# One transfer per 32 rows for an attention component's operands, and five adaLN blocks preloaded ahead of attention

## The reference, cut to what matters

```python
mod = silu(c) @ w_ada + b_ada                      # 6 x 1024 per sequence: "adaLN"
sh1, sc1, g1, sh2, sc2, g2 = split(mod, 6)
h   = rmsnorm(x, norm1_g) * (1 + sc1) + sh1
mix = concat[retention(h), forgetting_attention(h), differential_attention(h)]
x   = x + g1 * (mix @ w_out)
h   = rmsnorm(x, norm2_g) * (1 + sc2) + sh2
x   = x + g2 * (relu(h @ w_up) ** 2 @ w_down)

# differential attention, 6 heads of 2 x 32 query/key dimensions, both rotated (rope: halves of 16)
p = softmax(q[c] @ k[c].T / sqrt(32) + mask)       # c = 0, 1
a = p[0] - lam * p[1]
out = a @ v
```

## Time and profile before

| | us |
|---|---|
| median of three runs | 3327.64 |
| the profiled execution: own time | 3326.87 |
| the profiled execution: span, first to last instruction | 3325.1 |
| PE busy in it | 3224.1 (97%) |
| VectorE busy | 1696.0 (51%) |
| ScalarE busy | 984.5 (30%) |
| GpSimd busy | 957.8 (29%) |

### The profile page before, as it was taken

One profiled execution on the slowest core, in us unless ns is written; L12 is line 12 of the kernel. 1 busy time (PEld: TensorE's weight loads), 2 busy tenths in 40 slices (PEclk: granted clock), 3 DMA queues, 4 the chain that ended last, 5 costly groups with the idle time before them and its releaser, 6 DMA issues.

```text
span 3325.1 us, 50329 instructions
## 1 busy us (share of the span) xinstructions
PE 3224.1 (97%) x19286; PEld 2894.2 (87%) x19286; DVE 1696.0 (51%) x3073; ACT 984.5 (30%) x1770; POOL 957.8 (29%) x690
## 2 busy tenths in 40 slices
PE   6999999899999999999999999999999999999998
PEld 3988897566799999999988879966678999999997
DVE  4746273674495555555573544156546633333335
ACT  3132222574451111111232313147635311111112
POOL 1312332221232333333332214212213233333332
PEclk8999999999999999999999999999999999999999
DMA  5512476535112222222222114563321011111112
GB/s 213 180 47 95 156 238 218 125 91 139 33 59 85 85 76 76 88 82 82 83 64 73 35 50 176 190 172 76 76 66 45 27 51 44 44 45 50 44 44 72
DMA packets 135351, 307.07 MB, mean 92 GB/s; under 512 B 53789, under 2 KB 74341, under 8 KB 131729
## 3 DMA queue, kind: packets, MB, share of 16 engines
q1 hardware_dynamic: 93584, 224.39, 23.4%
q10 hardware_dynamic: 41600, 80.44, 6.9%
HBM read 240.14 MB, written 57.90 MB: 90 GB/s over the span
## 4 chain that ended last, share of the span: by engine, by line
PE 90%; DVE 4%; SPq 2%; ACT 1%; ACTq 1%; issue 1%; DMA 1%; DVEq 0%
PE ps L1387 22%; PE ps L1358 19%; PE ps L1299 9%; PE ps L1232 8%; PE ps L1022 6%; PE ps L1212 5%; PE ps L1078 4%; PE ps L1169 3%; PE ps L1276 3%; PE ps L1004 2%; PE ps L1046 1%; DVE tn L2053 1%; PE ps L1334 1%; DVE h_lo L2066 1%; DVE x L2238 1%; PE ps L1113 1%
## 5 line engine op out<-in xcount | busy, mean ns | idle before, releaser
L768 POOL CAST w_hi<-raw 128x1024 fp32r<-128x1024 f32 x212 | 229.5, 1082 | 1862.5 <-PEq L1393 447.3
L2238 DVE SCALAR_TENSOR_TENSOR x<-ps,mod,x 128x352 f32<-128x352 f32 (+2 forms) x768 | 353.6, 489 | 431.5 <-PE ps L1387 351.5
L1387 PE MATMUL ps<-act_hi,w_hi 128*128 128x352 f32 x1536 | 496.0, 323 | 0.0
L1387 PE MATMUL ps<-act_hi,w_lo 128*128 128x352 f32 x1536 | 492.6, 321 | 0.0
L1387 PE MATMUL ps<-act_lo,w_hi 128*128 128x352 f32 x1536 | 492.1, 320 | 0.0
L1358 PE MATMUL ps<-h_hi,w_hi 128*128 128x352 f32 x1344 | 433.5, 323 | 0.0
L1875 ACT ACTIVATE relu_b<-ps,consts 128x352 f32<-128x352 f32 x192 | 106.4, 554 | 1103.5 <-PE ps L1358 1084.3
L1358 PE MATMUL ps<-h_hi,w_lo 128*128 128x352 f32 x1344 | 430.8, 320 | 0.0
L1358 PE MATMUL ps<-h_lo,w_hi 128*128 128x352 f32 x1344 | 430.4, 320 | 0.0
L1299 PE MATMUL ps<-pT,vb 128*128 128x512 f32 (+5 forms) x1080 | 401.3, 461 | 0.0
L2302 DVE TENSOR_REDUCE pm<-ps 128x1 f32<-128x512 f32 (+4 forms) x468 | 251.2, 548 | 243.3 <-PE ps L1169 158.8
(11 more groups left out here) (223 smaller groups left out, 6112.3 us busy)
## 6 DMA issues: line engine op xcount, KB each, us to landing
raw<-in_w SPq DMA_DIRECT2D x212, 512.0 KB, 3.6
ada_next<-in_w_ada SPq DMA_DIRECT2D x48, 512.0 KB, 4.2
ada_w<-in_w_ada SPq DMA_DIRECT2D x24, 512.0 KB, 5.9
kb<-scr_k SPq DMA_DIRECT2D x36, 328.0 KB
kb<-scr_k SPq DMA_DIRECT2D x120, 82.0 KB
qb<-scr_q SPq DMA_DIRECT2D x36, 264.0 KB
ada_nat<-in_w_ada_first SPq DMA_DIRECT2D x8, 1024.0 KB, 20.5
qb<-scr_q SPq DMA_DIRECT2D x120, 66.0 KB
```

What stands on the lines that cost most here:

```text
L768: pool.tensor_copy(hi, raw[:, uc % 2, 0:width]).then_inc(pool_hi, 1)
L1387: last = mm(ps[:, i % 6, 0:GW], w[:, k * 256 + o * 128:k * 256 + o * 128 + 128], (act_lo if low else act_hi)[:, k * T + g * GW:k * T + (g ...
L2238: last = v.scalar_tensor_tensor(xs, ps[:, bank, a - g * GW:b - g * GW], gs, xs, ALU.mult, ALU.add)
```

## The change

```diff
-STACK_DMAS = {2: 14, 1: 9}
+STACK_DMAS = {2: 8, 1: 9}
...
-ADA_AFTER = {11: range(8, 10), 12: (10,), 13: (11,), 14: range(12, 19)}
+ADA_AFTER = {11: range(8, 10), 12: (10,), 13: (11,), 14: range(12, 19), 16: range(19, 22)}
...
-                    def part(src, which, y):
-                        r = 64 * y + 16 * a
-                        return src[n, which, r:r + 16]
+                    def part(src, which):
+                        return src[n, which].rearrange("(y b r) t -> b y r t", y=2, b=4)[a]
...
-                    for y in range(2):
-                        r = 16 * y
-                        sp.dma_start(k[r:r + 16, :].bitcast(F32), part(scr_k, 0, y)).then_inc(sem, 16)
-                        sp.dma_start(k[32 + r:48 + r, :].bitcast(F32), part(scr_k, 1, y)).then_inc(sem, 16)
-                        sp.dma_start(k[64 + r:80 + r, :].bitcast(F32), part(scr_k, 0, y)).then_inc(sem, 16)
-                        sp.dma_start(q[r:r + 16, 0:T].bitcast(F32), part(scr_q, 0, y)).then_inc(sem, 16)
-                        sp.dma_start(q[32 + r:48 + r, 0:T].bitcast(F32), part(scr_q, 0, y)).then_inc(sem, 16)
-                        sp.dma_start(q[64 + r:80 + r, 0:T].bitcast(F32), part(scr_q, 1, y)).then_inc(sem, 16)
+                    def rows32(buf, r, w):
+                        return buf[r:r + 32, 0:w].bitcast(F32)
+
+                    sp.dma_start(rows32(k, 0, NKEY), part(scr_k, 0)).then_inc(sem, 16)
+                    sp.dma_start(rows32(k, 32, NKEY), part(scr_k, 1)).then_inc(sem, 16)
+                    sp.dma_start(rows32(k, 64, NKEY), part(scr_k, 0)).then_inc(sem, 16)
+                    sp.dma_start(rows32(q, 0, T), part(scr_q, 0)).then_inc(sem, 16)
+                    sp.dma_start(rows32(q, 32, T), part(scr_q, 0)).then_inc(sem, 16)
+                    sp.dma_start(rows32(q, 64, T), part(scr_q, 1)).then_inc(sem, 16)
...
-                    if li == 0 and u < 8:
-                        sp.wait_ge(ada_done, 2 * (19 + u) + 2)
-                        back_load(24 + u)
+                    if li == 0 and u < 5:
+                        sp.wait_ge(ada_done, 2 * (22 + u) + 2)
+                        back_load(27 + u)
```

## The result

| | before | after |
|---|---|---|
| median of the runs, us | 3327.32 (3326.74 to 3330.47, 4 runs) | 3494.49 (3491.3 to 3498.27, 4 runs) |
| the profiled execution: span | 3325.1 | 3489.5 |
| PE busy in it | 3224.1 (97%) | 3257.2 (93%) |
| mean granted clock | 0.985 | 0.965 |

The ratio is 1.0501, with a 95% interval from 1.0483 to 1.0519: the changed kernel is 5% slower. Forecast were 3448 us and slower; direction and mechanism are right, the size is not: +164.4 between the two spans where the sum gave +120.8.

What follows compares the result with a forecast made beforehand. PE, busy 97%, was taken to bound the kernel, its standstills and lower clock moving the end. Projections +46.2, layer 0 +35.8 and layer 1 +38.8 gave +120.8 us on 3326.87: 3448 us, range 3375 to 3545.

Steps and rivals of the forecast that it cites:

- Two engines: Operand loads of the differential components: each new transfer runs on two of 16 DMA engines, 26.4 GB/s each.
- Term 1: End of the projections, both layers: weight unit 32 lands late behind operands, PE waits 23.1 us a layer, +46.2 in all.
- Term 2: First wait of attention: component 2's operands land late, a wait of 15.6 us in place of 5.3, +10.3 a layer.
- Term 3: Components 3 to 11: nine periods at 18.0 or 18.7 us in place of 14.3, +33.3 in layer 1, +39.6 in layer 0.
- One sign: Attention: PE would wait at L1169 for `kb`/`qb` in each of components 2 to 11.
- the values: Value loads in attention: 656 KB every fourth component, 1/16 on each engine, priced at 0.4 us a component.
- The clock: Attention: PE's lower-clock losses after the old waits would come back as gains, 4.8, 2.2 and 2.0 us.
- Part 2: The adaLN preload, layer 0: blocks 24 to 26 loaded early remove a 9.9 us wait and 2 us of lower clock.
- block 27: An adaLN load in layer 0's attention, needed in component 5, when the queue has just passed it; no cost priced.
- The first: Rival on the operand transfers: all 16 engines carry them, so issue time counts, -27.5, 3299 us; chance 0.12.
- the third rival: Component 2's wait stays since stores fill the engines, only the adaLN wait goes, -12, 3315 us; chance 0.03.
- The second: Rival in attention: two engines, ScalarE's queue held up too, PE waits for exponentials, 3528 us; 0.08 with a still slower engine.

Runs made afterwards that it cites:

- Experiment 1: The changed kernel with the 16 rows of a half outermost on each operand transfer's DRAM side, the two halves inside: 3309.01 us, ratio 0.9949.
- experiment 4: The kernel before, its 16-row operand transfers cut to a DRAM-side outermost count of 8, 4 or 2: 3351.5, 3381.1 and 3534.7 us.
- the doses of 2 and 4: The kernel before, its 16-row operand transfers given a DRAM-side outermost count of 2 or 4: 3534.7 and 3381.1 us.
- Experiment 6: The changed kernel with the value loads of pairs 2 to 5 cut to 16 of 128 rows: 3485.25 us, ratio 1.0476.
- experiment 2: The kernel before with only the adaLN edits: blocks 24 to 26 loaded after weight unit 32, 27 to 31 in the loop: 3325.76 us, ratio 0.9997.
- experiment 3: The changed kernel with the adaLN loads as before, so the merged 32-row transfers alone: 3533.37 us, ratio 1.0624.
- the two better versions: Experiment 1's kernel, 3309.01 us, and the same with ScalarE's last projection stores at slot 10 of component 0 in place of slot 3, 3301.29 us.
- experiment 9: The two better versions with the adaLN lines of the kernel before: 3310.38 us beside 3309.01, and 3312.76 us beside 3301.29.
- experiment 5: The changed kernel with the value loads of pairs 1 to 5 issued by ScalarE's queue in place of SP's: 3552.9 us, ratio 1.0674.

## Why the prediction was right, and where its size was off

**Two engines: right.** A 2 outermost on the DRAM side gives two engines' worth of work, at 27 GB/s each (26.4 were taken from the earlier trace rows, and the 21.1 of the earlier trace rows did not come). Experiment 1 takes the loss away with the order alone, experiment 4 brings it back without the merging. The Trainium skill, "DMA: Bandwidth & Descriptors", section "Why a DMA increments its semaphore by 16 and not by 1", has the rule for it: the largest count up to 16 that divides the slowest dimension of both sides. After, experiment 1 (16 and 32) and the doses of 2 and 4 agree with it; with 8 the engines are not full, so that its time neither bears the rule out nor speaks against it. The advice of the same page's "Rules for kernel authors", to coalesce small transfers, holds here only with the 16 outermost: the same merging gives -17 us with it and +206 without.

**Term 1: right.** 23.1 us were said for each layer, PE waits 24.0 and 24.6; unit 32 was to land at 544.9, and GpSimd starts on it at 545.13. The bounds of 10 and 31 were wider than needed.

**Term 2: right in kind, 4 us short.** A wait of 15.6 was said, 20.05 and 19.97 were measured. ScalarE's stores take more of the engines than the 5.0 us that I read from 8 us of before's queue: from 577 to 610 in after they are 22.2% of 33 us, 7.3 us on each engine. The rest may be the time by which the loads were issued one behind the other; no run separates it.

**Term 3, the period: right.** 18.0 was said, SP issues a component in 17.4 to 17.7. In undisturbed components the lag grows by 2.9 to 3.5 us (layer 1: components 5 to 8), against 3.7 forecast, 0.4 of them for the values. But there are eight such periods and not nine: component 11 adds nothing. The eight are some 25 us of the 59 in layer 1. One sign came otherwise than said: PE does not wait at L1169 in each component, but six times in all. In most components its stops of 1.0 to 2.6 us are at L1276, for row transfers. The loads set the pace even so: the chain of after from 600.17 to 662.95 holds SP's issues of operands and values and then the landing of `qb<-scr_rows` (646.70 to 662.95), and no work of an engine.

**The step that failed: the values.** The prediction says "A share of the values (656 KB every fourth component, 1/16 on each engine) adds 0.4 us": it priced them by bytes, and by a transfer that lands at once. Measured in layer 1, by what each component adds to the lag: component 4, after whose operands the values of pair 1 are issued, 8.9 us; components 9 and 10, at the values of pair 2, 13.9 and 5.7. Over the 3.2 of an ordinary component that is 5.7 and 13.2, 18.9 us a layer, where 3.6 were priced. Layer 1 missed by 59.2 - 38.8 = 20.4 us: 15.3 from the values, 4.8 from the start up to component 2 (4.4 of them the wait of term 2), 4.8 from the clock (below), less 4.5: 3.3 for component 11, and the rest since the other eight were a little cheaper than said. Two causes lie behind the values:
- The load is dearer than its bytes. It is read in pieces of 64 floats, 256 B. Queue of SP in the DMA view of 627 to 642 in after, where pair 1's values are loaded:

```profile
q1 hardware_dynamic: 2482, 1.34, 30.2%
```

  30.2% of 16 engines for 15 us are 72.5 us of engine time. Less 30 for the two that never rest, 42.5 us lie on the other 14: 3.0 us an engine for one load, and not 1.6 (a few constants of the operands are in the sum too). Cutting the loads of pairs 2 and 3 to an eighth gave back 4.0 us from component 0 to 11 of layer 1, and 1.4 in layer 0.
- It lands late. Pair 2's values are issued from 748 on, behind the operands of component 10, and wanted at 755.7, with the last of them landing 17.8 us after the first issue. In before the same six transfers went out from 654.20 and had landed by 660.0, 34 us ahead of PE's use at 694.5. So the lead is gone, and a part of each transfer lies behind a component's worth of operands on two engines: PE stands 10.1 us in layer 0 and 7.2 in layer 1. Experiment 6 shows that this stays with smaller loads and a free SP. It is 7.2 of the 13.2 us of layer 1. The remaining 6.0 go with what follows that stop, a lower clock (0.72 from 745.7 to 776.3 in layer 0) and a wait of 3.8 us for the next row transfer; no run takes them apart, nor the 5.7 us of pair 1, whose loads stayed whole in experiment 6.

**The clock: wrong.** The sum took 9.0 us off (4.8, 2.2 and 2.0), since clock losses would be hidden in stretches that the engines bind. But PE's busy time rose by 33.1 us with the same instructions: behind each wait PE runs at its lower level (1.2 GHz) for a part of the time, and there are many more waits (the granted clock was 0.90 in the steady period and 0.79 from 575 to 600, shown above; 0.985 and 0.965 over the spans). The first matmuls on unit 32 take 0.49 us and not 0.32. Within a late stretch this is hidden; at its start and end it is not: from component 0 to 2 of layer 1 the lag grows by 15.1 us, and the wait alone by 14.6. The 4.8 us are not returned there, nor later, as the rest of the lag is accounted for by the periods.

**Part 2: the forecast of -12 held only in company.** The wait at 600 is gone. Alone the edit gives nothing (experiment 2), beside the merged transfers 39 us (experiment 3), with the two better versions 1.4, within their spread, and 11.5 (experiment 9). What the prediction held hidden, block 27 "when the queue has just passed it", is late by 3.3 us for VectorE and 4.9 for PE: it is issued at 684.87, behind component 7's operands, and used at 702.74. That is part of layer 0's miss: component 6 adds 9.3 us to the lag, where an ordinary one adds about 3.

**Rivals.** The first (all 16 engines, 3299 us) is the case of experiment 1, with another order: 3309.0. It was 10 us too good, since the wait for component 2 stayed; the third rival had that half right (stores fill the engines). The second (ScalarE's queue held up too) did not happen as described: these small issues take 0.74 us (median) as before, and PE does not wait for exponentials. With larger transfers on that queue it does (experiment 5). But the row transfers land later, which no part of the prediction priced. One of them stands in the chain of after with

```profile
777.04 7.18 DMA qb<-nm_row
```

where before's chain has one of 3.72 us. PE waits 27.7 us for them in 15 places, and 1.1 us in one place before. A row transfer goes to 9 engines; that the two full ones are among them is inferred, no row shows it. In experiment 1 PE has no wait for `qb<-nm_row` at all.

## What to carry to other kernels

When a transfer is rewritten with more dimensions, read off the outermost count on each side before counting issues: merging 12 transfers into 6 moved the time by -17 us with 16 outermost and by +206 us with 2 outermost (both without the preload), and the two differ in the order of one view. Read the length of one issue too: fewer transfers of a longer form save less than their count says (4.65 us a component in place of 6.2). If a PE that waits for loads stands beside a DMA share far below 1, look for transfers on few engines, and expect everything behind them to be late, wide transfers and other issuers included. And price waits that follow each other together: the preload was worth nothing, nothing, 11.5 and 39 us beside four forms of the kernel.

## What the runs showed of the hardware that I had not expected

- An issue can last some ten microseconds while two engines behind it are full: 10.32 and 10.52 us for an 8 KB transfer on SP's queue, 11.54 and 13.01 us on ScalarE's, where the same issue (L638) took 0.62 us in before (median of 24; 4.05 at most). In experiment 5 ScalarE's issue stood although the operands that filled the two engines were on SP's queue; a 256 KB load that ScalarE had issued just before was in its own queue, and how much of the stop is due to that is not shown.
- An issue with one dimension more on the DRAM side took SP 0.59 to 0.65 us and not 0.42, with engines free.
- While SP stood in such an issue, the two engines went on at 56 GB/s together: a long issue shows a backlog, and taking it away (experiment 6) moved the landing by 0.1 us.
- A load's landing depends on the least free of its engines: the values of pair 2, spread over all, landed 17.8 us after their first issue (5.8 before), although 14 engines did next to nothing for some 8 us of it.
- The same held for the small row transfers: 7.18 us on the chain for 4.5 KB.
